# Feed-forwards 2 to 4 of a two-block transformer kernel: passes of two pairs, second-matrix units in twos between the pairs

## The reference

```python
# first block, l = 0, 1                       (feed-forwards 1 and 2)
f = (jax.nn.silu(h @ ffn_w1[l]) * (h @ ffn_w3[l])) @ ffn_w2[l]
x = x + g2 * f
# second block, i = 0, 1                      (feed-forwards 3 and 4)
gate, up = jnp.split(x @ w_ffn_in[i], 2, axis=-1)
ffn = (jax.nn.silu(gate) * up) @ w_ffn_out[i]
x = layer_norm(ALPHA * x + ffn + ple, ln2_g[i], ln2_b[i])
```

## Time and profile before

| | |
|---|---|
| median of 3 runs | 2541.24 us (2536.46 to 2541.75) |
| the profiled execution | 2539.25 us, span 2537.5 us |
| tensor engine busy | 2453.0 us, 97% of the span |
| vector engine, ACT, GpSimd busy | 62%, 41%, 41% |
| mean granted clock of the tensor engine | 0.988 |

### The profile page before, as it was taken

How to read it: one execution, slowest core, us unless ns; L and a number is a source line. 1 busy time by engine, 2 the same in 40 slices (tenths; PEclk the granted TensorE clock), 3 DMA queues, 4 the chain that set the end, 5 groups by cost and what they waited for, 6 DMA issues and landing times.

```text
span 2537.5 us, 32793 instructions
## 1 busy us (share of the span) xinstructions
PE 2453.0 (97%) x12859; PEld 2019.3 (80%) x12859; DVE 1584.6 (62%) x2380; ACT 1051.1 (41%) x1719; POOL 1038.1 (41%) x591
## 2 busy tenths in 40 slices
PE   7999999999999999999999999999999999999997
PEld 4777788888776787988677779898867777888896
DVE  5686877864487783644586476363568747645456
ACT  4335532333426542434443554343444355433342
POOL 0333453534325353435153355433514534553441
PEclk8999999999999999999999999999999999999998
DMA  8614335543222342332331213333323212333331
GB/s 283 200 50 133 117 133 183 189 159 102 86 82 94 122 131 89 103 94 99 102 84 58 67 65 102 100 96 104 100 81 83 75 50 67 99 101 100 100 100 50
DMA packets 239250, 268.73 MB, mean 106 GB/s; under 512 B 19592, under 2 KB 203640, under 8 KB 238840
## 3 DMA queue, kind: packets, MB, share of 16 engines
q1 hardware_dynamic: 239096, 266.63, 32.5%
HBM read 264.51 MB, written 2.10 MB: 105 GB/s over the span
## 4 chain that ended last, share of the span: by engine, by line
PE 79%; DVE 11%; ACT 3%; issue 3%; DMA 2%; POOL 1%; SPq 0%; ACTq 0%; DVEq 0%; POOLq 0%
PE bank L2730 24%; PE bank L2732 24%; PE bank L2731 24%; DVE r L1846 2%; DVE m_cv L2181 1%; DVE k_lo L1995 1%; POOL w_lo L1591 1%; DMA b_raw<-in_ada_w 1%; PE bank L3355 1%; ACT w_hi L992 1%; ACT k_hi L1046 1%; PE bank L3388 1%; DVE u_t_raw L2026 1%; DMA raw<-in_ffn_w 1%; PE bank L3050 1%
## 5 line engine op out<-in xcount | busy, mean ns | idle before, releaser
L1602 POOL TENSOR_TENSOR k_lo<-raw,k_hi 128x512 fp32r<-128x512 f32 x288 | 400.6, 1403 | 710.2 <-ACT k_hi L1046 707.3
L1046 ACT ACTIVATE k_hi<-raw 128x512 fp32r<-128x512 f32 x528 | 323.8, 627 | 471.2 <-PE bank L2732 371.8
L1591 POOL TENSOR_TENSOR w_lo<-raw,w_hi 128x2048 fp32r<-128x2048 f32 x53 | 248.1, 4681 | 534.1 <-ACT w_hi L992 452.7
L2730 PE MATMUL bank<-h_hi,k_lo 128*128 128x512 f32 (+1 forms) x1240 | 430.8, 347 | 3.8 <-DVE k_lo L1995 2.6
L2731 PE MATMUL bank<-h_lo,k_hi 128*128 128x512 f32 (+1 forms) x1240 | 429.4, 346 | 0.0
L2732 PE MATMUL bank<-h_hi,k_hi 128*128 128x512 f32 (+1 forms) x1240 | 429.1, 346 | 0.0
L2730 PE MATMUL bank<-h_hi,w_lo 128*128 128x512 f32 x800 | 323.0, 404 | 8.7 <-DVE h_lo L1955 3.9
L2732 PE MATMUL bank<-h_hi,w_hi 128*128 128x512 f32 x800 | 313.2, 391 | 0.0
L2731 PE MATMUL bank<-h_lo,w_hi 128*128 128x512 f32 x800 | 313.1, 391 | 0.0
L2730 PE MATMUL bank<-f_hi,k_lo 128*128 128x512 f32 x704 | 278.3, 395 | 10.3 <-DVE u_row L2054 8.3
L2731 PE MATMUL bank<-f_lo,k_hi 128*128 128x512 f32 x704 | 275.6, 391 | 0.0
(11 more groups left out here) (395 smaller groups left out, 4452.8 us busy)
## 6 DMA issues: line engine op xcount, KB each, us to landing
...
```

What stands on the lines that cost most here:

```text
L1046: act.activation(hi, src, ACT.Copy).then_inc(s.f_hi.up, 1)
L1591: pool.tensor_tensor(b.w_lo[p][:, 0:n], b.raw[p][:, 0:n], b.w_hi[p][:, 0:n].bitcast(F32), ALU.subtract)\
L1602: pool.tensor_tensor(lo, src, hi.bitcast(F32), ALU.subtract).then_inc(s.f_lo.up, 1)
L2730: pe.matmul(out, wlo, xhi, start=start, stop=False)
```

## The change

Feed-forward 1 keeps its units. In 2, 3 and 4 the passes are pairs 0-1, 2-3, 4-5, 6-7 and 8-10 (`SPREAD`). Behind each of pairs 3 to 10 stand the next two down units: the first pass's four behind pairs 3 and 4, the second's behind 5 and 6, and so on; the last pass's four are the tail, now of three slots each. So there are 20 down units instead of 12, of two slots (three in the tail); the matmuls are the same in number and form. Each adds two tiles to x.

The first down unit of two uses banks 2, 3 and the second 6, 7; plain units use 2, 3 for even pairs and 6, 7 for odd ones; the tail 0, 1 and 2, 3 by turns. In these feed-forwards the vector engine also takes M6 and M5 and the second slot of a down unit, and GpSimd makes every low part of u_full. Waits for banks are now one for each bank (`bank_taken`), in a seven just ahead of the bank's first product. `dve_sums` for a seven stands one slot ahead of the conversion of its M6 (behind the low parts of that turn), or three where there are two sets of sums, as in feed-forwards 3 and 4. A kind "upper" is defined, which no plan uses. The rest of the diff passes the plan on to the semaphores' counts.

```diff
@@ -55,10 +55,12 @@
 
 PAIRS = FF // G
 PASSES = [range(0, 4), range(4, 7), range(7, PAIRS)]
+SPREAD = [range(0, 2), range(2, 4), range(4, 6), range(6, 8), range(8, PAIRS)]
 AHEAD = [0, 1, 0]
 SPARE = 5
 RING = 8
 M1, M6, M7, M5, M4, M2, M3 = range(7)
+SEVENS = "seven", "upper"
 LAST_SLOTS = [(0, 1, 2, 3), (4, 5, 6, 7)] * 2
 
 
@@ -71,14 +73,19 @@
 
 
 
-    def __init__(self, early):
-        self.units, done = [], 0
-        for n, pairs in enumerate(PASSES):
-            upto = pairs[-1] + 1 + AHEAD[n]
-            for i in range(done, upto):
-                self.units += [("plain", i, 0), ("whole" if early and i == 0 else "seven", i, 0)]
-            done = upto
-            self.units += [("down", n, j) for j in range(KD // 2)]
+    def __init__(self, early, spread, uppers=(), sets=(1,)):
+        self.units, self.spread, self.sets = [], spread, sets
+        self.passes = SPREAD if spread else PASSES
+        downs = [("down", n, j) for n in range(len(self.passes)) for j in range(KD // 2)]
+        upto = {pairs[-1] + AHEAD[n]: KD // 2 for n, pairs in enumerate(PASSES)}
+        if spread:
+            upto = {i: 2 for i in range(3, PAIRS)}
+        for i in range(PAIRS):
+            self.units += [("upper" if i in uppers else "plain", i, 0),
+                           ("whole" if early and i == 0 else "seven", i, 0)]
+            self.units += downs[:upto.get(i, 0)]
+            del downs[:upto.get(i, 0)]
+        self.units += downs
         self.tail = len(self.units) - KD // 2
         self.early = early
         self.seq = [(u, n) for u in range(len(self.units)) for n in range(self.count(u))]
@@ -94,35 +101,51 @@
             at = max(at, self.before[q])
             self.after[at].append(q)
         self.mine = [self.on_vector(u, n) for u, n in self.seq]
+        self.summed = {}
+        for u, (kind, _, _) in enumerate(self.units):
+            if kind in SEVENS and self.at[u, M6] >= RING:
+                t = next(t for t, qs in self.after.items() if self.at[u, M6] in qs)
+                self.summed[t - (3 if kind == "seven" and len(sets) > 1 else 1)] = u
 
     def count(self, u):
         kind, n, _ = self.units[u]
-        return {"seven": 7, "whole": 4, "plain": 4}.get(kind) or len(PASSES[n])
+        return {"seven": 7, "upper": 7, "whole": 4, "plain": 4}.get(kind) or len(self.passes[n])
 
     def on_vector(self, u, n):
         kind = self.units[u][0]
+        if self.spread and kind != "plain":
+            return u >= 2 and u < self.tail and (n == 1 if kind == "down" else n not in (M1, M7))
         return u >= 2 and (kind == "plain" or (kind == "seven" and n in (M2, M4, M3)))
 
     def banks(self, u):
-        kind, i, _ = self.units[u]
+        kind, i, j = self.units[u]
         if kind == "seven":
-            return 0, 1, 4, 5
-        first = (6 if (i % 2 == 1) != (i >= len(PASSES[0])) else 2) if kind == "plain" else 2 * (u % 2)
+            return 0, 4, 1, 5
+        if kind == "upper":
+            return 2, 6, 3, 7
         if kind == "whole":
             first = 0
+        elif kind == "plain":
+            first = 6 if (i % 2 == 1) != (i >= len(PASSES[0]) and not self.spread) else 2
+        else:
+            first = 2 * (u % 2) if not self.spread or u >= self.tail else 6 if j % 2 else 2
         return first, first + 1
 
-    def sums(self, u):
-
-        return self.units[u][0] == "seven"
+    def pair_units(self, i):
+
+        return [u for u, x in enumerate(self.units) if x[0] != "down" and x[1] == i]
 
     def gate_done(self, u):
 
         return self.units[u - 1][1] if u and self.units[u - 1][0] in ("seven", "whole") else None
 
-    def nth(self, i):
-
-        return sum(kind == "seven" and j < i for kind, j, _ in self.units)
+    def nth(self, u):
+
+        return sum(kind in SEVENS for kind, _, _ in self.units[:u])
+
+    def sums(self, b, u):
+
+        return b.sums[self.sets[self.nth(u) % len(self.sets)]]
 
     def end(self, u):
         return max(q for q, x in enumerate(self.seq) if x[0] == u)
@@ -132,7 +155,7 @@
         return self.mine[q], sum(m == self.mine[q] for m in self.mine[:q + 1])
 
 
-PLAN = {1: Plan(True), 2: Plan(False)}
+PLAN = [Plan(True, False), Plan(True, True)] + [Plan(False, True, (), (2, 1))] * DEPTH
 UNITS = {1: 10 + 4, 2: 9 + 4 + 5}
 UNIT0 = {1: 0, 2: DEPTH * UNITS[1]}
 
...
@@ -701,23 +723,25 @@
     return buf[:, :].rearrange("p (k c) -> p k c", k=KD)
 
 
-def quarter(b, i, j):
-
-    return b.raw[1][:, :].rearrange("p (k j i c) -> p j i k c", j=2, i=2, c=P)[:, j, i]
+def quarters_of(b, u):
+
+    w = b.raw[u % 2][:, :].rearrange("p (k j i c) -> p j i k c", j=2, i=2, c=P)
+    return [w[:, j, i] for i, j in ((0, 0), (0, 1), (1, 0), (1, 1))]
 
 
 def by_tile(x):
     return x.rearrange("p (k c) -> p k c", c=P)
 
 
-def stationary(b, blk, plan, q):
+def stationary(b, plan, q):
 
     u, n = plan.seq[q]
     hi, lo = b.k_hi[:, plan.slot[q], :], b.k_lo[:, plan.slot[q], :]
-    if plan.units[u][0] != "seven":
+    if plan.units[u][0] not in SEVENS:
         return b.raw[u % 2][:, n * T:(n + 1) * T], hi, lo
-    s1, s2, s4 = (x[:, :] for x in b.sums[blk])
-    src = {M1: quarter(b, 0, 0), M2: quarter(b, 0, 1), M4: quarter(b, 1, 1), M7: quarter(b, 1, 0),
+    s1, s2, s4 = (x[:, :] for x in plan.sums(b, u))
+    a11, a12, a21, a22 = quarters_of(b, u)
+    src = {M1: a11, M2: a12, M4: a22, M7: a21,
            M5: by_tile(s1), M6: by_tile(s2), M3: by_tile(s4)}[n]
     return src, by_tile(hi), by_tile(lo)
 
...
@@ -1033,16 +1059,16 @@
 
     s, b, plan, n = e.s, e.b, lay.plan, lay.ffn
     u, part = plan.seq[q]
-    kind, i, _ = plan.units[u]
+    kind = plan.units[u][0]
     if q >= RING:
         act.wait_ge(*s.f_step(n, plan.before[q] + 1))
     else:
         act.wait_ge(*s.slot_free(lay.ffn_pair, q // 4))
-    if kind == "seven" and part in (M5, M6, M7, M3):
-        act.wait_ge(*s.f_sum(n, 4 * plan.nth(i) + {M5: 1, M6: 2, M7: 3, M3: 4}[part]))
+    if kind in SEVENS and part in (M5, M6, M7, M3):
+        act.wait_ge(*s.f_sum(n, 4 * plan.nth(u) + {M5: 1, M6: 2, M7: 3, M3: 4}[part]))
     else:
         act.wait_ge(*s.f_in[u % 2](n, 16 * (u // 2 + 1)))
-    src, hi, _ = stationary(b, lay.blk, plan, q)
+    src, hi, _ = stationary(b, plan, q)
     act.activation(hi, src, ACT.Copy).then_inc(s.f_hi.up, 1)
 
 
...
@@ -1623,7 +1650,7 @@
                 .then_inc(s.fl.up, 1)
 
     for t, (u, part) in enumerate(plan.seq):
-        if part == 1 and plan.gate_done(u) is not None and plan.units[u][0] != "down":
+        if part == 1 and plan.gate_done(u) is not None and (plan.spread or plan.units[u][0] != "down"):
             hidden(plan.gate_done(u))
         for q in plan.after[t]:
             pool_low(pool, e, lay, q)
...
@@ -1999,13 +2026,12 @@
 
 
     s, b, plan, n = e.s, e.b, lay.plan, lay.ffn
-    _, i, _ = plan.units[u]
-    s1, s2, s4 = (by_tile(x[:, :]) for x in b.sums[lay.blk])
-    a11, a12, a21, a22 = (quarter(b, *x) for x in ((0, 0), (0, 1), (1, 0), (1, 1)))
+    s1, s2, s4 = (by_tile(x[:, :]) for x in plan.sums(b, u))
+    a11, a12, a21, a22 = quarters_of(b, u)
     dve.wait_ge(*s.f_in[u % 2](n, 16 * (u // 2 + 1)))
-    i = plan.nth(i)
-    if i:
-        old = max(v for v in range(u) if plan.units[v][0] == "seven")
+    i = plan.nth(u)
+    if i >= len(plan.sets):
+        old = next(v for v, x in enumerate(plan.units) if x[0] in SEVENS and plan.nth(v) == i - len(plan.sets))
         dve.wait_ge(*s.low_in(n, plan, plan.at[old, M5]))
         dve.wait_ge(*s.low_in(n, plan, plan.at[old, M3]))
     dve.tensor_tensor(s1, a21, a22, ALU.add).then_inc(s.f_sum.up, 1)
...
@@ -2080,20 +2113,20 @@
         last = t == plan.end(u)
         if part == 0 and plan.gate_done(u) is not None:
             gated(plan.gate_done(u))
-            if kind == "down":
+            if kind == "down" and not plan.spread:
                 hidden_low(plan.gate_done(u))
         if u >= plan.tail:
             break
-        if kind == "seven":
-            parts(u, i, part)
-        if part == (M5 if kind == "seven" else 0) and u + 2 < plan.tail and plan.units[u + 2][0] == "seven":
-            dve_sums(dve, e, lay, u + 2)
+        if kind in SEVENS:
+            parts(u, kind, i, part)
         if kind == "down" and last:
             for m in range(2):
                 down(u, 2 * j + m, m)
         for q in plan.after[t - 1] if t else ():
             if plan.mine[q]:
                 dve_low_part(dve, e, lay, q)
+        if t in plan.summed:
+            dve_sums(dve, e, lay, plan.summed[t])
         if last and after is not None:
             after(u)
 
...
@@ -2857,34 +2891,44 @@
         return three(pe, bank[plan.banks(u)[m]][:, :], b.k_hi[:, at, v], b.k_lo[:, at, v], x[0][:, tile, :],
                      x[1][:, tile, :], start, stop)
 
-    def banks_free(u):
-
-
-        before = [v for v in range(u) if set(plan.banks(v)) & set(plan.banks(u))]
+    def bank_taken(u, at):
+
+
+        x = plan.banks(u)[at]
```

(78 more changed lines are left out.)

70 lines of the change are left out of this document (37 added, 33 removed).

## The result

The changed kernel takes 2699.23 us (median of 4 runs, 2690.87 to 2699.82), before 2539.53 us (4 runs, 2536.46 to 2541.75): a ratio of 1.0622, 95% interval 1.0598 to 1.0647, some 160 us slower. The profiled execution was the quickest, 2690.87 us with a span of 2689.1, so the traces are compared on a difference of 151.6 us. Its mean granted clock was 0.971, against 0.967 in the other three and 0.988 before.

A forecast was written before the change was run, and what follows sets the result against it. The tensor engine's stream of products was taken as the bound, so added waits set the loss: 54.6 us each in feed-forwards 3 and 4, 22.1 in 2, together 131.3 on 2539.25, forecast 2671; range 2595 to 2715, own range 2645 to 2700.

The forecast's parts named there:

- 3 even stalls: Feed-forwards 3 and 4: behind pairs 4, 6, 8 the first down unit stalls 8.2 us each for the gate.
- 4 odd stalls: Feed-forwards 3 and 4: behind pairs 3, 5, 7, 9 the second down unit stalls 2.8 us each.
- pair 10: Last pair, no next seven: its first down unit waits 3.0 us for banks, plus 0.9 of clock.
- 3 plains: Plain units 5, 7, 9 wait 0.9 us each for an x update to free banks 6, 7.
- Part 1 (banks): Behind even pairs the first down unit waits for banks 2, 3 until the gate: at least 3.0 us each.
- Parts 2 and 3 (late loads, sums): Late weight loads hold queues: even stalls 4.6 us in feed-forward 2; waiting sums make 8.2, odd 2.8, in 3 and 4.
- the upper bound: Sums of the next seven taking 4.8 us beside GpSimd instead of 2.6: 2.2 us more at seven places.
- Part 4 (clock): Half-clock matmuls after stalls: 1.7 us behind stalls of 4.6 and 8.2, 0.9 behind pair 10's, nothing behind 2.8.
- The rival that every stall pays: Every idle time drops the clock like the 3.7 us one: 2688, or 2719 with contended sums; chance 0.15.
- Part 5 (tails): Feed-forwards 3 and 4: tail's first slot held, 2.3 us; mean's chain late for last matmuls, 4.0 plus 0.8 clock.
- Part 6 (what goes): Feed-forward 2's u_row wait goes, 5.4 us back, 1.7 stays at pair 3's gate; feed-forward 1 loses nothing.
- vector engine as bound: Vector-engine waits pile up over a pair, each gate some 2 us later at 19 stalls: 2711 and more; chance 0.05.

The follow-up runs named there:

- Run 5: The changed kernel, but plain units and sevens of feed-forwards 2 to 4, from unit 2 on, load only an eighth of their weights: 2640.7 us.
- run 6: The changed kernel with only an eighth of those weights loaded and the sums one slot ahead of their use: 2626.7 us.
- Run 1: The changed kernel, but behind even pairs the first down unit uses banks 6, 7 and the second 2, 3: 2624.6 us.
- run 2: The changed kernel, but the sums of feed-forwards 3 and 4 stand one slot ahead of their use instead of three: 2652.9 us.
- run 7: The changed kernel with other banks behind even pairs, sums one slot ahead, and the tail's slots shifted by one in feed-forwards 3 and 4: 2564.6 us.
- run 8: The changed code with the old order of units in all four feed-forwards and the sums ahead of the low parts of their slot: 2553.2 us.
- run 9: The changed code with the old order of units and the sums where the kernel before has them, behind the weighing: 2544.0 us, ratio 0.9999.

## Why the prediction came out, and where it was short

The direction and the mechanism held: 18 gate waits over 2.5 us where 11 or more were named as the sign, nine x waits of 0.83 or 0.89 in the places named, the two slot waits and the two for the mean. The size was short: the sum was 131.3 us on the profiled execution, and it grew by 151.6; the median, 2699.2, lies at the top of the forecast's own range (2645 to 2700). By the ends of the feed-forwards: the first lost 4.5 (predicted nothing), the stretch to the second's end 24.4 (22.1), to the third's 59.3 and to the fourth's 63.5 (54.6 each).

| feed-forward 3 | predicted | measured |
|---|---|---|
| 3 even stalls | 24.6 | 8.67 + 8.31 + 8.91 = 25.9 |
| their clock | 5.1 | 12 matmuls from 1672.96 to 1677.92 in 4.96, at full clock 2.73: 2.2 each, 6.7 |
| 4 odd stalls | 11.2 | 3.07 + 2.84 + 2.76 + 2.35 = 11.0, and 1.7 of clock behind one |
| pair 10 | 3.0 + 0.9 | 2.9, and 9 matmuls to 1906.33 in 3.72 for 2.05: 1.7 |
| 3 plains | 2.7 | 2.5 |
| tail, slot | 2.3 | 2.3 |
| tail, mean | 4.0 + 0.8 | 3.0 + 1.8 |

The measured column gives 59.5 of the 62.1; the other 2.6 are not placed.

**Part 1 (banks)** held: 0.83 at the plains, 2.88 at pair 10, and runs 5 (in feed-forward 2) and 6 (in all three) show the bare 2.88 behind even pairs too. Run 1 confirms that the bank decides when the stall begins.

**Parts 2 and 3 (late loads, sums)** held step by step. With 0 at 1658.65 the steps were forecast at 5.3, 8.4, 11.0, 12.45 and 13.7; they came at 5.5, 8.9, 11.5, 12.9 and 14.2. Run 5 comes within 1 us of its forecast, which is luck in part, as its four executions lie 10.5 us apart; run 2 comes within 10. The delay of the second load had been read off two loads 0.4 us apart and used for two 1.7 apart: 6.7 us from issue to landing, where 7.2, 6.8 and 7.4 were measured. The sums took 2.54 here (1667.59 to 1670.13), not the 4.8 of the upper bound. Feed-forward 2's even stalls were 4.63, 4.78 and 4.50 for 4.6.

**Part 4 (clock)** is the term of the sum that was mis-sized. Behind the 4.5 to 4.8 us stalls of feed-forward 2 it cost 1.5 to 1.6 us, near the 1.7 charged. Behind the 8.2 to 9.0 us stalls of 3 and 4 it cost 2.1 to 2.7, since 9 to 12 starts lay 0.427 us or more apart, where the 1.7 had been read off some 8. And the waits near 3 us were not free: of the eleven gate waits of 2.3 to 3.1 in feed-forwards 2 to 4, four had 6 or 7 starts 0.427 apart behind them, 1.6 to 1.7 us each, two of those behind odd pairs, which I had at nothing. The rival that every stall pays did not occur either: seven had none. The Trainium skill (TensorE: Matmul & The Clock Gate, section HAM oscillation) describes a kernel whose wait for its next operand, some 3 to 5 us, drops the clock anew ahead of every short burst of matmuls. The traces agree for the longer waits, all nine gate waits of 4.5 us and more in the change; of the shorter ones, 4 of 11 in the change and 10 of 12 in run 6 dropped it too.

**Part 5 (tails)**: the slot's 2.27 to the hundredth, and run 7 shows its cause. The mean's chain was late by 3.0, not 4.0; its clock of 1.8 evened that out.

**Part 6 (what goes)** failed for feed-forward 1. "Feed-forward 1 keeps its order but for the sums one conversion later: nothing" overlooked that for pair 8 the sums move a slot forward and across the weighing of the modulation piece, in a queue that works in the written order: runs 8 and 9. The wait for u_row did get 1.3 shorter, what is waited for b_raw 4.0 longer, and 2.0 came from slower running. Pair 3 of feed-forward 2 waits 1.74 for the 1.7 forecast, and 1.16 for x on top.

The distance of the median (28 above 2671) is thus 4.5 from feed-forward 1; 2.3 from feed-forward 2, where seven x waits took 4.9 us and 3.0 was forecast; 13.7 from 3 and 4 with the mixers ahead of them, clock for the most part; and 8.4 by which the median lies above the profiled execution, the others having a clock 0.004 lower (my estimate of what that is worth, 0.4% of 2689, is 11). The *vector engine as bound* rival counted 19 stalls; its own list has 20, and none of them shows the 2 us more.
